# GpSimd's subtractions over prepared weights, issued as one instruction each instead of two to four pieces

## The reference

```python
# first block, layer 1: neighbourhood attention ("na"), 16 heads of 64
q_l, k_l, v_l = jnp.split(h_lat @ w_qkv, 3, axis=-1)
q_c, k_c, v_c = jnp.split(h_ctx @ w_qkv, 3, axis=-1)
p = softmax(concat([q_r @ k_win + bias, q_r @ k_c]));  o = p @ [v_win, v_c]
...
# second block, each of two layers
proj = rms_norm(x) @ w_in                      # gates, "mla", "rwkv" and "conv" columns
o_a = causal attention over low-rank q, k, v   # mla, 8 heads
o_b = rwkv7 scan                               # 4 heads of 64
o_c = short convolution
x = x + (g0 * o_a + g1 * o_b + g2 * o_c) @ w_out
x = x + square(relu(rms_norm(x) @ w_up)) @ w_down
```

## Time and profile before

| | |
|---|---|
| median of 3 runs | 4269.67 us (4261.37 to 4270.57) |
| the profiled execution's own time | 4261.37 us |
| its span in the profile | 4259.6 us |
| PE busy | 3857.9 us, 91% |
| DVE busy | 1835.2 us, 43% |
| ACT busy | 1324.2 us, 31% |
| POOL busy | 456.7 us, 11%, 379 instructions |

### The profile page before, as it was taken

One profiled execution on the slowest core, in us unless ns is written; L12 is line 12 of the kernel. 1 busy time (PEld: TensorE's weight loads), 2 busy tenths in 40 slices (PEclk: granted clock), 3 DMA queues, 4 the chain that ended last, 5 costly groups with the idle time before them and its releaser, 6 DMA issues.

```text
span 4259.6 us, 52528 instructions
## 1 busy us (share of the span) xinstructions
PE 3857.9 (91%) x21392; PEld 3013.5 (71%) x21392; DVE 1835.2 (43%) x2812; ACT 1324.2 (31%) x1963; POOL 456.7 (11%) x379
## 2 busy tenths in 40 slices
PE   7788878999998999899978889899998798989999
PEld 3555546788886787688865667678886566767887
DVE  2544443533334334444434354544333435454333
ACT  3332322322223323323333431233232333123222
POOL 0211110000002211000021230000011122000000
PEclk9878889999998999899989999999999999999999
DMA  4112243121111222232211221032321121113322
GB/s 162 53 48 80 90 170 108 50 70 60 60 53 57 80 95 85 74 102 92 89 46 34 68 57 40 30 106 90 99 85 41 43 74 50 33 39 108 96 93 69
DMA packets 320320, 317.03 MB, mean 74 GB/s; under 512 B 8720, under 2 KB 286128, under 8 KB 319952
## 3 DMA queue, kind: packets, MB, share of 16 engines
q1 hardware_dynamic: 320080, 313.67, 23.3%
HBM read 311.55 MB, written 2.10 MB: 74 GB/s over the span
## 4 chain that ended last, share of the span: by engine, by line
PE 78%; DVE 11%; ACT 5%; DMA 2%; issue 2%; POOL 1%; DVEq 0%; SPq 0%; ACTq 0%; POOLq 0%
PE PS L132 78%; DVE scr L146 5%; ACT scr L142 3%; DMA ring<-in_ada_w 1%; DVE scr L156 1%; DVE scr L164 1%; DVE PS L160 1%; ACT L142 1%; PE PS L135 1%; DVE NBt L156 1%; DVE scr L168 1%; POOL ring_r L146 1%; POOL NBt L146 0%; DVE scr L176 0%; DVE scr L152 0%
## 5 line engine op out<-in xcount | busy, mean ns | idle before, releaser
L132 PE MATMUL PS<-scr 128*32 128x32 f32 (+7 forms) x6692 | 648.1, 279 | 144.9 <-DVE scr L146 69.6
L132 PEld LDWEIGHTS PS<-scr 128*128 128x128 f32 (+4 forms) x6692 | 529.2, 167 | 291.2 <-issue 119.6
L132 PE MATMUL PS<-ffn_h,ffn_w 128*128 128x512 f32 (+1 forms) x3168 | 616.2, 357 | 7.8 <-DVE ffn_h L156 5.7
L132 PEld LDWEIGHTS PS<-ffn_h,ffn_w 128*128 128x128 f32 x3168 | 524.7, 190 | 100.5 <-issue 9.1
L142 ACT ACTIVATE scr<-PS 128x256 f32<-128x256 f32 (+5 forms) x425 | 193.2, 455 | 820.8 <-PE PS L132 752.6
L132 PE MATMUL PS<-h_h,ring_r 128*128 128x512 f32 (+1 forms) x976 | 356.6, 428 | 38.2 <-POOL ring_r L146 24.3
L142 ACT ACTIVATE scr<-scr 128x256 f32<-128x256 f32 (+7 forms) x404 | 212.6, 526 | 519.9 <-DVE scr L156 322.3
L132 PE MATMUL PS<-mlp_h,mlp_w 128*128 128x512 f32 x1536 | 361.3, 396 | 0.0
L132 PE MATMUL PS<-mlp_g,mlp_w 128*128 128x512 f32 x1536 | 359.7, 396 | 0.0
L132 PEld LDWEIGHTS PS<-mlp_h,mlp_w 128*128 128x128 f32 x1536 | 288.4, 188 | 70.5 <-issue 1.0
L132 PEld LDWEIGHTS PS<-mlp_g,mlp_w 128*128 128x128 f32 x1536 | 288.5, 188 | 69.9
(11 more groups left out here) (151 smaller groups left out, 4736.6 us busy)
## 6 DMA issues: line engine op xcount, KB each, us to landing
ring<-in_ada_w SPq DMA_DIRECT2D x48, 1024.0 KB, 6.1
ring<-in_ffn_w_in SPq DMA_DIRECT2D x44, 1024.0 KB, 5.0
ring<-in_w_up SPq DMA_DIRECT2D x32, 1024.0 KB, 5.5
ring<-in_w_down SPq DMA_DIRECT2D x32, 1024.0 KB, 5.0
ring<-in_w_in SPq DMA_DIRECT2D x60, 512.0 KB, 3.9
ring<-in_ffn_w_out SPq DMA_DIRECT2D x16, 1024.0 KB, 5.1
scr<-in_na_bias SPq DMA_DIRECT2D x32, 512.0 KB, 5.0
ring<-in_na_w_qkv SPq DMA_DIRECT2D x24, 512.0 KB, 4.2
```

The lines of the kernel that those rows point to most:

```text
L132: return self.eng.matmul(o, lhsT=l, rhs=r, start=start, stop=stop) if self.eng else Nothing()
```

## The change

Each of the three helpers issued its subtraction in pieces, of 512 columns (`split_pool`, `halve_pool`) or of 672 (`m_in_pool`), each with its own semaphore update and each waiting for the piece before. Now each issues a single instruction over the whole tile. PE waited for the last piece before, and waits for the one instruction now. Nothing else differs: the same elements are read and written, the loads, ACT's copies, and the programs of PE, DVE, ACT and SP are the same.

```diff
-            for c in range(0, n, 512):
-                cs = slice(c, c + 512)
-                pool.tt(lo[:, cs], raw(("na" + p, tl), n)[:, cs], hi[:, cs].bitcast(F32), ALU.subtract).then_inc(
-                    *(pool.up("na_lo") if c + 512 < n else pool.up("na_lo", p, tl)))
+            pool.tt(lo, raw(("na" + p, tl), n), hi.bitcast(F32), ALU.subtract).then_inc(*pool.up("na_lo", p, tl))
...
-        for c in range(0, n, 512):
-            m = min(n - c, 512)
-            pool.tt(ringr[:, o + c:o + c + m], raw(key, n)[:, c:c + m], ringr[:, o + 1024 + c:o + 1024 + c + m].bitcast(F32),
-                    ALU.subtract).then_inc(*(pool.up("t_lo", *key) if c + m == n else pool.up("t_lo")))
+        pool.tt(ringr[:, o:o + n], raw(key, n), ringr[:, o + 1024:o + 1024 + n].bitcast(F32), ALU.subtract).then_inc(*pool.up("t_lo", *key))
...
-        w = raw(("m_in", l, j), 672 * nk).rearrange("p (k c) -> p k c", k=nk)
-        for k in range(nk):
-            pool.tt(wl[:, k, :], w[:, k, :], wh[:, k, :].bitcast(F32), ALU.subtract).then_inc(
-                *(pool.up("t_lo") if k < nk - 1 else pool.up("t_lo", "m_in", l, j)))
+        pool.tt(wl, raw(("m_in", l, j), 672 * nk).rearrange("p (k c) -> p k c", k=nk), wh.bitcast(F32), ALU.subtract).then_inc(*pool.up("t_lo", "m_in", l, j))
```

## The result

The changed kernel took 4294.44 us (median of 5 runs, 4287.54 to 4297.92). The kernel before took 4269.67 us in the five runs beside it (4261.37 to 4279.02). The ratio is 1.0057, with a 95% interval of 1.0039 to 1.0075: 25 us slower, where 23 were forecast. The profiled execution took 4293.35 us.

The account below looks back on a forecast made before the run. PE was taken to bound the kernel (78% of the critical chain, DVE 11%, POOL 1%). Terms without the clock sum to +17.2 us; with +6 for PE's clock, +23.2 on 4269.7 gives 4293 us, range 4268 to 4316.

Parts of the forecast that it names:

- the turns: Six turns of the neighbourhood attention: +15.0 us from later `dg`, plus +6 us from PE's slower clock.
- the opening: Start of the attention: `na_l` ends later behind POOL's longer first instruction, +2.0 us; second `na_w` wait shorter, -0.8.
- the entry to the second block: PE's wait for POOL's sums of squares: one instruction of 4.4 us brings them forward, -0.9 us.
- all behind it: After the second block's entry: `ring_r` gates -1.3, last mla items +2.2, rwkv stage +1.0 us (ends -3 and +4).
- The hold: In each turn `dg` waits for POOL's whole 4.5 us instruction, 3.09 us late; PE 2.50 later, +15.0 over six.
- the TENSOR_SCALAR's gain: In each turn the small TENSOR_SCALAR behind `dg` no longer waits for POOL: 0.17 instead of 0.76 us, 0.59 saved.
- The rival on the other side: POOL does not hold DVE off through a long instruction, so `dg` passes: -9.6 us, 4260 us; chance 0.08.
- taken in: Rival: ACT's exponentials or loads bound the next items and absorb the turns' delay; +2 remains, 4272 us; chance 0.10.
- The clock: Longer PE idle in the turns drops its clock to 0.50, 1.7 us per stretch: +6 us, from 0 to 10.2.
- the second wait: PE's other wait for `na_w`, 1.6 us in the opening, shortens by 0.8 us.
- The last mla item: Last item of the mla attention: `dg` loses its seam and PE waits, +1.1 us in each of two layers, +2.2.
- The waits on `ring_r`: PE's five waits, 24.3 us in all, each behind a POOL pair that shortens by 0.3 us: -1.3 us.

Follow-up runs that it names:

- fill_pe: only_na plus three fp32 matmuls on PE in each turn's idle time before its wait for `dg`: 4286.04 us, ratio 1.0036.
- only_rest: Kernel after with `split_pool` put back to pieces of 512; `halve_pool` and `m_in_pool` stay one instruction each: 4275.31 us, ratio 1.0016.
- only_na: Kernel before with only `split_pool` (the attention's weight tiles) issuing one instruction per tile: 4291.72 us, ratio 1.0056.
- two_1024: Kernel before with `split_pool` in pieces of 1024 columns instead of 512: 4268.78 us, ratio 1.0005.
- cuts_1408: Kernel before with the qk tiles of the six turns in three pieces (512, 896, 640 columns) instead of four of 512: 4263.85 us, ratio 0.9985.
- cuts_all: Kernel before with v, second qk and second block's input tiles merged, six turns' qk tiles cut into 512, 832, 704 columns: 4258.97 us, ratio 0.9976.
- late_start: only_na plus a POOL wait meant to start the qk subtraction later, but on the wrong item, so the start did not move: 4287.97 us, ratio 1.0051.
- p256: Kernel before with the attention's weight tiles in pieces of 256 columns instead of 512: 4271.5 us, ratio 1.0005.
- late_start2: only_na plus a POOL wait for the turn's own TENSOR_SCALAR, starting the long instruction behind `dg`: 4269.25 us, ratio 1.0004.

## Why the prediction was right

By the profiles, the whole is 32.0 us, of which 4.8 were there before the changed code ran, so 27.2 us for a forecast of 23.2. Part by part: the turns 20.2 for 21.0 (hold and clock together), the opening -0.1 for +1.2, the entry to the second block -0.6 for -0.9, all behind it 7.7 for 1.9. The mechanism was right; the match of the sum owes something to luck, as the following shows.

*The hold* was the step on which all rested, and it came out almost exactly: `dg` was to take about 3.5 us and took 3.54, ending 0.28 us behind POOL (0.27 was read from the earlier trace rows, at less than half the length). 2.50 us a turn were forecast net of the TENSOR_SCALAR's gain; fill_pe shows 2.54 with the clock out of the way. The rival on the other side, a hold given up within a long instruction, is refuted by all six turns, and the delay was not taken in anywhere: the 34.44 us of dense PE work merely moved.

*The clock* came out at 5.0 us for +6, but not by the way assumed. I had put 1.7 us on each of some 3.5 turns, as if dense matmuls lay in the slow stretch. It fell in all six turns; what lay in the stretch was `flip` and the gaps around it, so it cost 0.5 to 0.9 us in the first five (the turns' 44.53 to 44.95 less 44.06) and the rest, 1.9 us, in the sixth with its 6.83 us. Two errors, too few turns and too much for each, met in one sum: that the term fits is luck. PE's one piece of idle time was also put too long, at 3.3 us; it was 2.69, from the end of a few small matmuls at 1484.73.

*The opening* was mis-sized as a whole, by a term that it lacked, the clock. +2.0 for `na_l` and -0.8 for the second wait were forecast. The two rows of the kernel after:

```profile
1349.40 4.51 POOL L146 TENSOR_TENSOR na_w<-ring,na_w 128x2048 fp32r<-128x2048 f32 x1 [5.88 <-ACT na_w L142]
...
1351.87 2.97 DVE L156 SCALAR_TENSOR_TENSOR na_l<-NBt,MODt,na_h 128x512 fp32r<-128x512 f32 x1 [0.71 <-ACT na_h L142]
```

`na_l` came 1.8 us later, as forecast. PE's matmuls at 1390 (before) were 2.4 us later than at 1340, and the first behind the second wait, 1398.09 before and 1404.46 after, 0.8 less, as forecast. But from 1340 to 1412 the kernel in sum neither lost nor gained (4.8 to 4.7 us). The remaining 1.6 us came back from the clock: before, a stretch at 0.50 from 1394.80 to 1401.63 covers the first projections behind the second wait; after, PE ran the same matmuls at 1.00 there. The windows over the two places, first before:

```profile
1394.80:1401.63 6.83, 5.16 (x16) 3.68 (x15) 4.13 (x12) 3.19 (x7) 3.08 (x3) 0.50 0.35 109
```

and after:

```profile
1402.84:1409.67 6.83, 5.21 (x24) 4.32 (x24) 3.84 (x10) 2.60 (x8) 1.57 (x1) 1.00 0.46 156
```

PE's waits for `na_w` fell from 6.6 us to 1.6, yet most of that changed its name only: its waits for `na_l` rose from 9.9 us to 15.4. The clock did not stand at full speed for longer in all: before, it was 0.50 from 1336.80 and from 1357.28 for 17.07 us each and for the 6.83 us shown, 40.97 us together; after, it was 0.50 in one piece from 1341.39 for 40.96 us. What changed is which matmuls fell under it.

*The entry to the second block*: forecast -0.9, measured -0.6. PE's row after, which answers to the earlier trace rows:

```profile
2172.04 3.12 PE L132 MATMUL PS<-KC,NBt 128*128 128x2 f32 x14 [9.60 <-POOL NBt L146]
```

*The last mla item*: forecast +1.1 in each layer. POOL, DVE and PE in the first layer, which answer to the earlier trace rows:

```profile
2452.93 2.34 POOL L146 TENSOR_TENSOR ring_r<-ring,ring_r 128x1024 fp32r<-128x1024 f32 x1 [17.43 <-ACT ring_r L142]
...
2453.57 1.98 DVE L146 TENSOR_TENSOR scr<-KC,scr 128x256 f32<-128x256 f32 x1
...
2455.60 2.05 PE L132 MATMUL PS<-scr 128*128 128x128 f32 x16 [2.67 <-DVE scr L146]
```

PE's wait grew from 1.57 to 2.67 us, so +1.1 as forecast; in the second layer the same `dg` went from 0.89 to 1.97 us. The waits on `ring_r` fell from 24.3 to 22.0 us, more than the 1.3 forecast. From 2152 to the end the kernel lost 7.7 us, against 1.9 forecast for gates, mla and rwkv. Here the profiles can't tell the code's cost from drift: only_rest, with the same code there, lost 4.1, but only_na and fill_pe lost 3.6 and 3.5 us with the old code. That there is a real cost is known from only_rest's median (1.0016, 1.0004 to 1.0028), which stands above the +1 us that the terms outside the attention add up to (-0.9, -1.3, +2.2, +1.0). Besides the last mla items, where it arises, and what the rwkv stage costs by itself, was not settled.

One statement was wrong without bearing on a number: the turn's `dg` is that of the fourth item of a head pair, not of the third.

The Trainium skill (SBUF — State Buffer, "Who interferes with whom") says of the pair of ports that "Whoever issues first gets the shared pair for the whole instruction", and holds an instruction of one SBUF input outside its faster modes to be free of it. The runs agree with the first: `dg` waited to the end of 1024 and 2048 columns alike. With the second they are in line, no more: a RECIPROCAL of 128x2 took 0.17 us in the middle of POOL's instruction, where a TENSOR_SCALAR of the same size had waited, and no trace here shows in which mode either ran.

## What to carry to other kernels

Where DVE and GpSimd run side by side, the length of a GpSimd instruction is the longest time for which it made a DVE instruction of the held kinds late here, and a seam between two pieces was the only place where such an instruction got in. So split by where the DVE instructions on the critical path arrive, not evenly and not as little as possible: two cuts in the right places in place of three even ones were worth 3 us in the six turns here, while no cut at all cost 20. Before a helper engine is made "more efficient", look at who runs next to it and whether that one is on the chain; and if a piece can't be split, start it right behind the instruction that must not wait, if its result has time enough.

## What the runs showed of the hardware

- The hold lasts to the end of GpSimd's instruction, at 2.1 us and at 4.5 us of length. A held product of 256 columns ends 0.27 to 0.28 us behind it, a held TENSOR_SCALAR of 128x2 0.02 to 0.03 us (before, two_1024, cuts_1408).
- Not every DVE instruction is held. In the turn after, the RECIPROCAL (128x2, 0.17 us) ran inside POOL's 4.51 us, and in cuts_all the maxima (CUSTOM_DVE_ANT_0, one input from PSUM and one from SBUF, 0.70 us) ran beside POOL as fast as without it. Held were products of two SBUF inputs and the TENSOR_SCALAR.
- A gap between two GpSimd instructions of under 0.1 us (1476.12 to 1476.20) is enough to let a DVE instruction in that stands ready, six times out of six in cuts_all, cuts_1408 and before.
- PE's idle time of 2.69 us ahead of `flip` was followed by a granted clock of 0.50 in six turns of six; the same six turns of only_na and of late_start show the same. Idle times of 1.6 us (before, ahead of `values`), 1.4 us (p256) and 1.0 to 1.1 us (late_start2, fill_pe, cuts_all) in these turns never were.
